# Paired attentions: probabilities transposed in two 64-row halves, one PSUM bank per half, with renumbered key tiles

## The reference

```python
def gqa_attend(q, k, v, bias=None, sink=None):      # head size 64
    s = jnp.einsum("bqhgd,bkhd->bhgqk", q, k) * ATTN_SCALE
    if bias is not None: s = s + bias
    if sink is not None: ...                        # one more column in the softmax
    p = jax.nn.softmax(s, axis=-1)
    return jnp.einsum("bhgqk,bkhd->bqhgd", p, v)
# A: 8 query heads over 2 key heads, 512 image queries over 768 keys, 256 context queries over 256 keys
# B: the same heads; a block of 128 image queries sees its band and the context (4 or 5 tiles of 128 keys)
# D: 8 heads, 512 queries, each block of 128 sees 2 tiles of image keys and 2 of context, with a bias table
```

## Time and profile before

| what | value |
|---|---|
| median of 3 runs | 1772.61 us (1768.92 to 1773.26) |
| span of the profiled execution | 1770.6 us |
| own time of the profiled execution | not given apart from its span |
| PE busy in the span | 97% |
| DVE, ACT busy | 56%, 42% |
| share of the two attention loops | 184 + 75 us |

### The profile page before, as it was taken

One profiled execution on the slowest core, in us unless ns is written; L12 is line 12 of the kernel. 1 busy time (PEld: TensorE's weight loads), 2 busy tenths in 40 slices (PEclk: granted clock), 3 DMA queues, 4 the chain that ended last, 5 costly groups with the idle time before them and its releaser, 6 DMA issues.

```text
span 1770.6 us, 24448 instructions
## 1 busy us (share of the span) xinstructions
PE 1716.5 (97%) x9338; PEld 1378.4 (78%) x9338; DVE 998.6 (56%) x2024; ACT 740.3 (42%) x1465; POOL 621.2 (35%) x272
## 2 busy tenths in 40 slices
PE   8999999899999999999999999999999999999997
PEld 6889777688888888888888876755568888896686
DVE  4799544542222455555695315666753667985563
ACT  5222354552333454444323441466753225225553
POOL 3776232252334454444464222100002233521142
PEclk9999999999999999999999999999999999999998
DMA  8566221132224223333563221100002442321031
GB/s 239 156 178 179 78 68 52 48 111 80 84 73 142 83 87 101 99 96 92 173 181 113 84 80 48 36 2 1 2 1 66 135 124 75 87 71 33 29 96 48
DMA packets 255154, 156.28 MB, mean 88 GB/s; under 512 B 6017, under 2 KB 250942, under 8 KB 255038
## 3 DMA queue, kind: packets, MB, share of 16 engines
q1 hardware_dynamic: 251518, 147.12, 28.5%
q10 hardware_dynamic: 3520, 7.60, 1.3%
HBM read 152.60 MB, written 2.10 MB: 87 GB/s over the span
## 4 chain that ended last, share of the span: by engine, by line
PE 89%; DVE 4%; ACT 3%; issue 2%; POOL 1%; DMA 1%; SPq 0%; ACTq 0%; DVEq 0%
PE ps L787 68%; PE ps L2423 4%; PE ps L2434 3%; PE ps L2455 3%; PE ps L1555 1%; PE ps L1519 1%; PE ps L1571 1%; POOL w_lo L768 1%; DMA mod_raw<-in_mod_w 1%; ACT w_hi L709 1%; PE ps L1563 1%; PE ps L2459 1%; PE ps L2171 1%; DVE pg L3132 0%; PE ps L1203 0%
## 5 line engine op out<-in xcount | busy, mean ns | idle before, releaser
L768 POOL TENSOR_TENSOR w_lo<-w_raw,w_hi 128x1024 fp32r<-128x1024 f32 (+1 forms) x220 | 565.2, 2574 | 1073.4 <-ACT w_hi L709 1073.0
L787 PE MATMUL ps<-h_hi,w_lo 128*128 128x512 f32 x1088 | 433.7, 399 | 10.5 <-DVE h_lo L1106 2.9
L787 PE MATMUL ps<-h_hi,w_hi 128*128 128x512 f32 x1088 | 424.7, 390 | 0.0
L787 PE MATMUL ps<-h_lo,w_hi 128*128 128x512 f32 x1088 | 424.4, 390 | 0.0
L787 PEld LDWEIGHTS ps<-h_hi,w_lo 128*128 128x128 f32 x1088 | 204.8, 188 | 59.9 <-issue 6.5
L709 ACT ACTIVATE w_hi<-w_raw 128x1024 fp32r<-128x1024 f32 (+1 forms) x220 | 228.7, 1045 | 39.8 <-PE ps L787 22.8
L787 PEld LDWEIGHTS ps<-h_hi,w_hi 128*128 128x128 f32 x1088 | 204.6, 188 | 43.9
L787 PEld LDWEIGHTS ps<-h_lo,w_hi 128*128 128x128 f32 x1088 | 204.8, 188 | 41.5 <-issue 1.4
L1504 DVE SCALAR_TENSOR_TENSOR mod_sums_odd<-mod_raw,small,mod_sums_odd 128x256 f32<-128x256 f32 x168 | 108.0, 714 | 0.0
L2511 ACT ACTIVATE probs<-probs,small 128x512 f32<-128x512 f32 (+3 forms) x128 | 93.3, 729 | 10.3 <-DVE small L2528 8.8
L2434 PE MATMUL ps<-ident,probs 128*128 128x128 f32 x528 | 84.0, 283 | 7.4 <-DVE probsT L2540 5.2
(11 more groups left out here) (425 smaller groups left out, 3294.8 us busy)
## 6 DMA issues: line engine op xcount, KB each, us to landing
w_raw<-in_w_in SPq DMA_DIRECT2D x56, 512.0 KB, 5.3
mod_raw<-in_mod_w SPq DMA_DIRECT2D x24, 1024.0 KB, 5.4
w_raw<-in_w_up SPq DMA_DIRECT2D x44, 512.0 KB, 3.8
w_raw<-in_od_w_in SPq DMA_DIRECT2D x28, 512.0 KB, 3.8
w_raw<-in_ev_w_in SPq DMA_DIRECT2D x20, 512.0 KB, 3.7
w_raw<-in_w_down SPq DMA_DIRECT2D x16, 512.0 KB, 4.0
w_raw<-in_w_mem_kv SPq DMA_DIRECT2D x8, 512.0 KB, 3.9
w_raw<-in_w_attn_branch SPq DMA_DIRECT2D x8, 512.0 KB, 3.7
```

The costliest lines, as they stand in the source:

```text
L768: POOL.tensor_tensor(wlo[:, p, 0:n], raw[:, p, 0:n], f(whi[:, p, 0:n]), ALU.subtract).then_inc(*chunk_lo.by(c))
L787: ins = PE.matmul(out, l, r, start=first and n == 0, stop=last and n == 2)
```

## The change

Before, the turn of a key tile is one transpose of 128 rows (queries) into 128 columns of PSUM. DVE's tiles go to bank 4 and ACT's to bank 5. Now each tile is turned by two transposes. One takes the rows 0 to 63 of the probabilities with the upper left quarter of the identity, the other the rows 64 to 127 with the lower right quarter; each gives 128 keys by 64 queries. All lower halves go to bank 4 and are DVE's to copy, all upper halves go to bank 5 and are ACT's. The inverse sums are transposed alike, the halves to banks 6 and 7, so that `pe_values` has two further waits: for ACT's copy of the inverse sums of the group before, ahead of the products, and for DVE's output of that group, ahead of these transposes. So that each unit's tiles lie side by side in `probsT`, the key tiles have new numbers (`KEY_BLOCK`, `order`).

```diff
-    def turned_to(probsT, p, s, part):
-        tiles, off = part, p % 2 * P
-        step = tiles[1] - tiles[0] if len(tiles) > 1 else 1
-        return probsT[s][p // 2 % 2][:, tiles[0]:tiles[-1] + 1:step, off:off + P]
+    def turned_to(probsT, p, s, u, half):
+        first, off = min(u["tiles"]), p % 2 * P + half * HEAD
+        return probsT[s][p // 2 % 2][:, first:first + len(u["tiles"]), off:off + HEAD]
+
+    def turned_from(u, half):
+        n = len(u["tiles"])
+        return bank(4 + half, n * HEAD).rearrange("p (k n) -> p k n", n=HEAD)
+
+    def halves_turned(half):
+        rows_ = slice(half * HEAD, (half + 1) * HEAD)
+        return rows_, ident[rows_, rows_]
...
-        at = 0
-        for b, part in ((4, u["dve"]), (5, u["act"])):
-            for k in range(len(part)):
-                ins = PE.transpose(bank(b, P, k * P), probs[s][p % 2][:, at:at + P], ident[:])
-                at += P
+        first = min(u["tiles"])
+        for n, k in enumerate(u["tiles"]):
+            for half in range(2):
+                rows_, own = halves_turned(half)
+                ins = PE.transpose(bank(4 + half, HEAD, (k - first) * HEAD), probs[s][p % 2][rows_, n * P:(n + 1) * P], own)
...
+        if g:
+            PE.wait_ge(*p_inv_copied(x_, g - 1))
...
         PE.wait_ge(*p_widened(x_, g))
+        if g:
+            PE.wait_ge(*p_attended(x_, g - 1))
         for n in range(2):
-            ins = PE.transpose(bank(b, P, (2 + n) * P), inv_wide[:, n, :], ident[:])
+            for half in range(2):
+                rows_, own = halves_turned(half)
+                ins = PE.transpose(bank(6 + half, HEAD, 2 * P + n * HEAD), inv_wide[rows_, n, :], own)
...
-            ACTE.activation(turned_to(probsT, p, s, part), bank(5, len(part) * P).rearrange("p (k n) -> p k n", n=P),
+            ACTE.activation(turned_to(probsT, p, s, us[p], 1), turned_from(us[p], 1),
...
-            DVE.tensor_copy(turned_to(probsT, p, s, part),
-                            bank(4, len(part) * P).rearrange("p (k n) -> p k n", n=P)).then_inc(*p_copied_dve.by(x_, p, s))
+            DVE.tensor_copy(turned_to(probsT, p, s, us[p], 0),
+                            turned_from(us[p], 0)).then_inc(*p_copied_dve.by(x_, p, s))
...
-        ACTE.activation(us[2 * g]["out"], bank(6 + g % 2, 2 * P, 2 * P), ACT.Copy).then_inc(*p_inv_copied.by(x_, g))
+        spread_at = ps[:, 6 * 512:8 * 512].rearrange("p (h e) -> p h e", h=2)[:, :, 2 * P:3 * P]
+        ACTE.activation(us[2 * g]["out"].rearrange("p (n h q) -> p h n q", n=2, h=2),
+                        spread_at.rearrange("p h (n q) -> p h n q", n=2), ACT.Copy).then_inc(*p_inv_copied.by(x_, g))
+
+    KEY_BLOCK = (2, 3, 0, 1, 4, 5)
...
-                        v=lambda k, s, kv=kv: v3[x_][:, k, kv * HEAD:(kv + 1) * HEAD])
+                        v=lambda k, s, kv=kv: v3[x_][:, KEY_BLOCK[k], kv * HEAD:(kv + 1) * HEAD])
```

More of the change, by code:

```diff
@@ L2441, in pe_values @@
         b = 6 + g % 2
-        first, second = set(u0["dve"] + u0["act"]), set(u1["dve"] + u1["act"])
+        first, second = set(u0["tiles"]), set(u1["tiles"])
         tiles = sorted(first & second) + sorted(first ^ second)
@@ L2485, in copy @@
         def copy(p, s):
-            part = us[p]["act"]
             ACTE.wait_ge(*p_turned(x_, p, s))
@@ L2535, in copy @@
         def copy(p, s):
-            part = us[p]["dve"]
             DVE.wait_ge(*p_turned(x_, p, s))
@@ L2592, in even_pairs, with pair @@
             base = dict(k=[(own[0] if s == kv else own[1])[s * HEAD:(s + 1) * HEAD, :] for s in range(2)],
-                        v=lambda k, s, kv=kv: v3[x_][:, k, kv * HEAD:(kv + 1) * HEAD])
+                        v=lambda k, s, kv=kv: v3[x_][:, KEY_BLOCK[k], kv * HEAD:(kv + 1) * HEAD])
             if x_ == "B":
                 base.update(sink=[sink[:, h:h + 1] for h in heads_], nsink=[nsink[:, h:h + 1] for h in heads_])
-            def pair(i, at, tiles, scores, dve, act, zero):
-                u = dict(base, n=tiles * P, scores=scores, dve=dve, act=act,
+            def pair(i, at, key_blocks, scores, zero):
+                tiles = len(key_blocks)
+                u = dict(base, n=tiles * P, scores=scores, tiles=[KEY_BLOCK.index(k) for k in key_blocks],
                          q=[qT3[x_][s * HEAD:(s + 1) * HEAD, n, at:at + P] for s in range(2)],
@@ L2607, in even_pairs @@
                 if x_ == "A":
-                    us.append(pair(i, at, 6, [(0, 512, 0), (512, 256, 512)], [0, 1, 2], [3, 4, 5], 0))
+                    us.append(pair(i, at, [0, 1, 2, 3, 4, 5], [(0, 512, 0), (512, 256, 512)], 0))
                 elif i == 0:
-                    us.append(pair(i, at, 4, [(0, 256, CTX), (256, 256, 0)], [2, 3], [0, 1], 3))
+                    us.append(pair(i, at, [2, 3, 0, 1], [(0, 256, CTX), (256, 256, 0)], 3))
                 elif i == NB - 1:
-                    us.append(pair(i, at, 4, [(0, 256, 0), (256, 256, CTX + (NB - 2) * P)], [0, 1], [4, 5], 0))
+                    us.append(pair(i, at, [0, 1, 4, 5], [(0, 256, 0), (256, 256, CTX + (NB - 2) * P)], 0))
                 else:
-                    us.append(pair(i, at, 5, [(0, 384, CTX + (i - 1) * P), (384, 128, 0), (512, 128, P)],
-                                   [i + 1, i + 2, i + 3], [0, 1], 2))
+                    us.append(pair(i, at, [i + 1, i + 2, i + 3, 0, 1],
+                                   [(0, 384, CTX + (i - 1) * P), (384, 128, 0), (512, 128, P)], 2))
             for i in range(CB):
-                us.append(pair(i, i * P, 2, [(0, 256, 0)], [0], [1], 0))
+                us.append(pair(i, i * P, [0, 1], [(0, 256, 0)], 0))
         return us
@@ L2973, in odd_pair @@
         inner = i < 3
-        img = [2 + i, 3 + i] if inner else [2, 5]
+        order = [[2, 3, 0, 1, 4], [4, 5, 0, 1, 2]][i // 2]
+        key_blocks = [0, 1, 2 + i, 3 + i] if inner else [2, 5, 0, 1]
         at = [(0, 256, 0), (256, 256, CTX + i * P)] if inner else [(0, P, CTX), (P, P, CTX + 3 * P), (256, 256, 0)]
         first = 2 * P if inner else 0
-        return dict(scores=at, n=4 * P, dve=[0, 1] if inner else img, act=img if inner else [0, 1],
+        return dict(scores=at, n=4 * P, tiles=[order.index(k) for k in key_blocks],
                     q=[dqT[s * HEAD:(s + 1) * HEAD, n, i * P:(i + 1) * P] for s in range(2)],
                     k=[dkT[s * HEAD:(s + 1) * HEAD, n, :] for s in range(2)],
-                    v=lambda k, s: dvt[:, k, (2 * n + s) * HEAD:(2 * n + s + 1) * HEAD],
+                    v=lambda k, s: dvt[:, order[k], (2 * n + s) * HEAD:(2 * n + s + 1) * HEAD],
                     bias=[dbias[(2 * n + s) % 4][:, first:first + 4 * P] for s in range(2)],
```

## The result

The changed kernel takes 1752.82 us in the median (1751.66 to 1754.61, 4 runs) beside 1770.76 (1768.91 to 1773.26, 4 runs) for the kernel before: the ratio is 0.9907, with a 95% interval of 0.9895 to 0.992. The forecast was 1754, counted from the 1772.61 that the kernel before had then in 3 runs. The profiled execution took 1752.38 us, with a span of 1751.0.

What follows compares the result with a forecast made beforehand. PE was taken to bound some steps of the attention loops, DVE's loop the others. Savings of 7.6 (A), 6.2 (B) and 4.6 (D), together 18.4 us, took 1770.6 to 1752.2; with 2.0 for the median, 1754 us, range 1748 to 1767.

Steps and rivals of the forecast that it cites:

- The bound: Attention loops: PE bounds some steps, DVE's loop of maximum, copy, maximum the others; only the first kind gain, down to that loop.
- A1 and A2: First two of six steps of a head pair in loop A: held at 4.03 us by DVE's loop, nothing saved.
- D1: First of two kinds of step in loop D: 3.04 to 2.95 us, DVE's bound, in 7 steps, 0.6 us.
- The tile: Turn of one key tile: two halves side by side cost 0.056 us for 0.109, 0.053 saved.
- A4: Fourth step of a head pair in loop A, bound by PE: 14 tiles, need 3.03 us, saves 0.98.
- D2: Second kind of step in loop D, 3.69 us, PE-bound: 8 tiles, need 3.03, saves 0.66 in 6 of 8, 4.0 us.
- B5: Fifth step of a head pair in loop B, bound by PE: falls to 2.37 us, saves 0.45.
- The joins: Changes of array shape between scores and turn fall away and the first load hides: 0.24 us a PE-bound step.
- The copies: DVE's and ACT's copies in pieces of 64: no visible cost; at 0.02 a piece, 3 us in all.
- Halves don't pay: Rival: tile stays at 0.109 us, only shape changes pay 8.1, 1764.5 us; chance 0.08, slower issue to 1772 another 0.06.
- Slower: Rival: second half's load waits for the first half's stream, 0.22 us a tile, 1816 us; chance 0.07.
- Partly hidden: Rival: a longer wait in the loop than scaled, by a copy or new wait, takes half: 1763 us; chance 0.16.

Runs made afterwards that it cites:

- the experiment by heads: Changed kernel, but ACT copies both halves of head 0 and DVE both halves of head 1: 1744.20 us, ratio 0.9865.
- the kernel with whole inverse sums: Changed kernel, but inverse sums transposed on 128 rows into one bank as before, without the two further waits: 1753.33 us, ratio 0.9914.
- the run with the lower rows alone: Changed kernel, but both transposes of a tile read rows 0 to 63: 1769.46 us, ratio 1.0002.
- the kernel with the masks moved: Changed kernel, but D's bias table loads, and with them GpSimd's mask additions, come one step earlier: 1751.69 us, ratio 0.9906.
- a different share of the copies: Changed kernel, but ACT copies head 0 and DVE head 1, sharing head 1 by halves before short scores: 1742.59 us, ratio 0.9847.

## Why the prediction was right

**The bound.** Right: A1 and A2 stayed where they were and B6 nearly (3.16 for 3.21), and the experiment by heads shortened these steps, with A3, A6 and B1 to B3, once DVE's loop was shorter. D's loop was put 0.06 too long: D1 is 2.89 where 2.95 was the bound. In the steps of 2.89 the first load of the scores hides behind the turn, so that the scores take 1.08 for 1.13 and the first maximum starts 1.13 behind them for 1.18; the forecast had hidden that load for PE and not for DVE.

**The tile.** Right in its mechanism, short in size: 0.062 in place of 0.056. The forecast took the stream of half a transpose as half of 0.11 and let the load of 0.06 hide behind it; the run with the lower rows alone shows one half transpose at 0.062. Which of load and stream sets that, no run here tells. It shows in the steps that PE bounds: A4 3.07 for 3.03, D2 3.05 to 3.10 for 3.03. B5 is 2.45 for 2.37, of which its four tiles explain 0.02; the rest stays open.

**The joins.** Right: turns of 6 start 0.21 behind the last scores, the stream alone, and the kernel with whole inverse sums brings a join back. A4 fell by 0.94; 14 tiles at 0.047 are 0.66 of it, which leaves 0.28 for the joins where the sum had 0.24.

**The copies.** That pieces of 64 cost nothing came true, but it didn't follow from the earlier trace rows: there a copy with three times the pieces also has three times the elements, so the two lengths can't tell a cost of a piece from one of an element. The changed kernel tells it: 555 and 288 ns with twice the pieces.

**The sum of A and B.** A head pair of A went from 23.44 to 21.64 us, 1.80 for a forecast 1.90. What is missing is A5: 2.75 where I took 2.65 without a row for it; A4 gave 0.04 less and A6 0.05 more. A pair of B went from 20.66 to 19.13, 1.53 for 1.56. The loop gave 13.6 of 13.8.

**The sum of D.** Forecast 4.6, measured 3.75 in the one profile and 5.5 in the other. The plain steps came as said or a little better: D2 3.70 and 3.69 to 3.07 and 3.10, D1 3.04 to 2.89 or 2.90 in three steps and to 2.94 or not at all in others. Two things that the sum had no term for lie over them. The first is the mask addition. GpSimd's additions and DVE's copies of the inverse sums in the changed kernel:

```profile
1604.90 3.60 POOL L3025 TENSOR_TENSOR bias<-bias,near_mask 128x768 f32<-128x768 f32 x2 [18.72 <-DMA bias<-in_rpb_rows]
1606.98 1.68 DVE L2585 COPY inv_wide<-small 128x256 f32<-128x256 f32 x1
1623.04 3.61 POOL L3025 TENSOR_TENSOR bias<-bias,near_mask 128x768 f32<-128x768 f32 x2 [14.54 <-DMA bias<-in_rpb_rows]
1625.50 1.30 DVE L2585 COPY inv_wide<-small 128x256 f32<-128x256 f32 x1
```

and in the kernel before, where I had not looked:

```profile
1619.38 3.61 POOL L3008 TENSOR_TENSOR bias<-bias,near_mask 128x768 f32<-128x768 f32 x2 [18.12 <-DMA bias<-in_rpb_rows]
1622.16 0.98 DVE L2574 COPY inv_wide<-small 128x256 f32<-128x256 f32 x1
1639.43 3.60 POOL L3008 TENSOR_TENSOR bias<-bias,near_mask 128x768 f32<-128x768 f32 x2 [16.44 <-DMA bias<-in_rpb_rows]
1642.59 0.59 DVE L2574 COPY inv_wide<-small 128x256 f32<-128x256 f32 x1
```

The copy takes 0.28 elsewhere. Here it ends at 1608.66, 1626.80, 1623.14 and 1643.18, each 0.15 us behind the end of the addition. Faster steps brought the copy to an earlier point of the addition, and the wait grew by 1.41 us in all: 4.21 became 4.69, and 3.70 only 3.52. The sum had 0.66 for the second and, if the first is the D2 that it left out as waiting beside other DVE work, nothing for that: 0.48 short in each, together about the 0.85 that is missing.

The second is the clock. The products of conv_y with ones, between the scores of the loop's second and third step, in the changed kernel, with a window in it (the granted clock is the third number from the right), and then in the kernel before:

```profile
1585.95 5.40 PE L3045 MATMUL ps<-conv_y,ones 128*128 128x512 f32 x8
1587.00:1590.40 3.40, 3.40 (x6) 1.40 (x5) 0.00 (x0) 0.15 (x2) 0.00 (x0) 0.54 0.52 154
```

```profile
1601.26 3.60 PE L3028 MATMUL ps<-conv_y,ones 128*128 128x512 f32 x8
```

At 0.54 TensorE is near the lower of its two levels, 1.2 GHz. In the other profile of the same kernel no such stretch fell there and they took 3.70: that is 1.7 us, just the difference between 70.08 and 68.34. But the kernel before had its stretch too, over the two steps of 7.76 and 5.60 us that became 6.47 and 4.66. A window in it, and then the whole loop of D in the second profile of the changed kernel:

```profile
1630.50:1637.30 6.80, 6.80 (x32) 5.25 (x33) 1.67 (x5) 0.43 (x2) 0.00 (x0) 0.50 0.01 2
```

```profile
1575.62:1643.96 68.34, 61.36 (x681) 46.14 (x680) 42.16 (x131) 41.46 (x112) 9.57 (x5) 0.98 0.10 32
```

The loop has a mean granted clock of 0.95 in the kernel before and in the first profile of the changed one, some 6.8 us at half clock in each, and 0.98 in the second, 3.4 us. So 3.75 is the fair measure of the change, short of the 4.6 by the mask addition, and the 5.5 has 1.7 us from the clock in it.

**The rest.** 2.3 us lie outside the loops, where the program is the same. The time ahead of the loop is 1129.28 before, 1127.75 in the changed kernel and 1126.37 to 1128.36 in the others. The forecast had nothing there. Half-clock stretches fall on other work in each execution, and behind the loop of D they go with the time: 106.1 us with 10.4 at half clock before, 105.4 with 7.2 in the changed kernel; of the others, two with 9.4 and 9.9 have 105.6 and 105.8, and the rest, with 6.7 to 7.5, 105.3 or 105.4. Ahead of the loops they don't: before has 13.7 us at half clock and the changed kernel 3.4, but the kernel with the masks moved has 13.7 as well and starts its loop at 1127.63, and two others with 6.8 at 1126.37 and 1128.36. So the cause of these 1.5 us is open. The median stands 1.8 above the profile's span, for the 2.0 that I added; an execution's time is 1.2 to 1.5 above its own span in every run, so the rest of either number is only that the median and the profiled execution are different ones. By luck, then, the 1754 came out within 1.2 us: the loops gave 1.1 us less than the sum, and the rest, for which it had no term, 2.3 more.

**The rivals.** *Halves don't pay* at 0.109 or 0.124 a tile fell; the run with the lower rows alone is that case, and takes as long as the kernel before. The fear behind it, that PE can't start a matmul every 0.028, fell too: 12 starts in 0.53 less 0.22 is one in 0.028. By the 62 ns a matmul that the Trainium skill states for matmuls decoded by the sequencer (TensorE: Matmul & The Clock Gate, Part 1), 11 distances would be an estimated 0.68; that is what one row half alone shows, and not both together, so the measurement decides against it as a limit of issue here. *Slower*, 0.22 a tile, had no part. *Partly hidden* fell with the copies' unchanged 555 and 288 ns and with waits that cost nothing.

## What to carry to other kernels

Transposes that fill the array's rows can be split by rows into halves that run side by side, here each into a bank of its own (one bank for both was not tried); it pays when the products around them have the halves' shape too, so that no change of shape is left, and only in steps that PE bounds. Before such an edit list the steps where PE is busy for the whole length, and find the loop that bounds the others: once PE was faster, a different share of the copies took another 10.3 us off the loop of A and B, beside the 13.6 of the change. Whether it would have paid before the change was not run. And look for what a shortened loop will meet: here a copy of 0.28 us that ran into another engine's addition and took up to 1.68.

## What was not expected of the hardware

- DVE's copy from SBUF to SBUF, 256 elements of float32, stood still until the running one of GpSimd's two additions of 768 had ended, 4 times of 4 here and 15 of 15 over all profiles, and ended 0.15 us behind it. Its addition with two operands in SBUF, 0.68 long, did the same once (2.29) and ended 0.55 behind. Both are the instruction's own length less 0.13, as if it waited whole and then ran whole. With the other order of starts it was GpSimd's addition that grew, 3.60 to 4.07. The Trainium skill (SBUF — State Buffer, Who interferes with whom) has the shared port pair of the two engines as an exclusive lock under which the second to issue fully blocks; the trace agrees. DVE's maxima, with scores from PSUM, were not longer beside the same additions, 0.67, nor were its output (L2591, one operand from PSUM), 0.42, and its reciprocals of 2 elements, 0.15.
- With all lower halves issued ahead of all upper ones, three pairs still ran side by side, so PE reaches about three transposes ahead to the idle row half. The Trainium skill (TensorE: Matmul & The Clock Gate, Part 3) has matmuls start strictly in the program's order; a turn of 6 would then need ten distances of 0.06, and the record shows eight (0.71 less 0.22). Which transposes the pairs are, the records don't name.
- One half transpose takes 0.062 us alone or in a pair, while a whole one took 0.11.
